# Transposes, ada outputs and row scales at new places in a two-block transformer kernel

## The reference

```
mod = silu(c) @ ada_w + ada_b                 # six rows: shift, scale, gate, twice
h = rmsnorm(x, g1) * (1 + scale_m) + shift_m
x = x + gate_m * token_mix(h)                 # gated linear attention, latent attention (16 heads), a gated sum, @ w_out
h = rmsnorm(x, g2) * (1 + scale_f) + shift_f
x = x + gate_f * ((silu(h @ Wg) * (h @ Wu)) @ w_down)
x = rmsnorm(x, final_norm_g)
```

```
proj = rms_norm(x, pre_g[l]) @ w_in[l]        # retention, differential attention, gated linear recurrence
mixed = [retention * silu, diff_attention * silu, lru * silu]
x = x + rms_norm(mixed @ w_out[l], post_g[l])
```

## Time and profile before

| | us |
|---|---|
| median of 3 runs | 2756.21 (2754.75 to 2757.06) |
| profiled execution | 2750.28 |
| its span | 2748.5 |
| mean granted TensorE clock | 0.989 of full |
| PE busy | 2605.1 |
| DVE, ACT busy | 1757.0, 1295.9 |

### The profile page before, as it was taken

One profiled execution on the slowest core, in us unless ns is written; L12 is line 12 of the kernel. 1 busy time (PEld: TensorE's weight loads), 2 busy tenths in 40 slices (PEclk: granted clock), 3 DMA queues, 4 the chain that ended last, 5 costly groups with the idle time before them and its releaser, 6 DMA issues.

```text
span 2748.5 us, 36054 instructions
## 1 busy us (share of the span) xinstructions
PE 2605.1 (95%) x13167; PEld 2202.0 (80%) x13167; DVE 1757.0 (64%) x2417; ACT 1295.9 (47%) x1885; POOL 69.8 (3%) x110
## 2 busy tenths in 40 slices
PE   2898999899999999899999999999999999999998
PEld 2787887788878778788888888888887887878886
DVE  5887776776666665677765555565666555566654
ACT  2334344534555444544443444445645544565553
POOL 0000000000000000000000000002000000200000
PEclk9999999999999999999999999999999999999999
DMA  9875666788656567577776666656565465656464
GB/s 338 281 258 175 192 192 189 222 280 282 210 179 191 181 223 224 183 256 248 246 230 194 190 188 186 189 179 174 158 185 167 124 220 142 182 161 181 134 198 140
DMA packets 341690, 554.82 MB, mean 202 GB/s; under 512 B 24590, under 2 KB 135932, under 8 KB 340876
## 3 DMA queue, kind: packets, MB, share of 16 engines
q1 hardware_dynamic: 335616, 541.79, 62.6%
q0 software_dynamic: 3280, 7.64, 0.9%
q10 hardware_dynamic: 2620, 3.09, 0.3%
HBM read 550.35 MB, written 2.10 MB: 201 GB/s over the span
## 4 chain that ended last, share of the span: by engine, by line
PE 81%; issue 6%; DVE 5%; ACT 4%; POOL 1%; DVEq 0%; POOLq 0%; ACTq 0%
PE gp L786 72%; PE tp L786 6%; PE tp L789 2%; ACT whi L1194 2%; DVE wlo L1771 1%; POOL stat L2429 1%; DVE acc L1777 0%; ACT rv L1194 0%; ACT L1194 0%; DVE xs L1777 0%; DVE xs L1771 0%; DVE m L1771 0%; DVE yd L1771 0%; DVE sgb L1771 0%; ACT stg L1194 0%
## 5 line engine op out<-in xcount | busy, mean ns | idle before, releaser
L1771 DVE TENSOR_TENSOR wlo<-raw,whi 128x1024 fp32r<-128x1024 f32 (+1 forms) x842 | 989.3, 1188 | 626.4 <-ACT whi L1194 624.5
L1194 ACT ACTIVATE whi<-raw 128x1024 fp32r<-128x1024 f32 (+1 forms) x842 | 852.1, 1029 | 571.3 <-PE gp L786 481.4
L786 PE MATMUL gp<-whi,h 128*128 128x512 f32 (+1 forms) x2944 | 929.4, 388 | 6.6 <-DVE wlo L1771 3.1
L786 PEld LDWEIGHTS gp<-whi,h 128*128 128x128 f32 x2944 | 551.8, 189 | 112.3 <-issue 15.8
L786 PE MATMUL gp<-h,whi 128*128 128x512 f32 (+1 forms) x1936 | 601.9, 370 | 23.4 <-DVE wlo L1771 16.6
L786 PE MATMUL gp<-wlo,h 128*128 128x512 f32 (+1 forms) x1472 | 561.2, 381 | 0.0
L786 PE MATMUL gp<-h,wlo 128*128 128x256 f32 x1680 | 473.6, 282 | 0.0
L786 PEld LDWEIGHTS gp<-h,whi 128*128 128x128 f32 x1936 | 352.8, 192 | 92.4 <-issue 25.7
L786 PEld LDWEIGHTS gp<-h,wlo 128*128 128x128 f32 x1680 | 320.6, 191 | 0.8 <-issue 0.7
L786 PEld LDWEIGHTS gp<-wlo,h 128*128 128x128 f32 x1472 | 278.0, 189 | 45.3 <-issue 1.4
L1777 DVE SCALAR_TENSOR_TENSOR acc<-raw,cact,acc 128x512 f32<-128x512 f32 x298 | 223.3, 749 | 11.4 <-DMA raw<-in_ada_w_dram 4.5
(11 more groups left out here) (318 smaller groups left out, 2704.3 us busy)
## 6 DMA issues: line engine op xcount, KB each, us to landing
raw<-in_w_in_dram SPq DMA_DIRECT2D x314, 512.0 KB, 4.4
raw<-in_ffn_w_in_dram SPq DMA_DIRECT2D x176, 512.0 KB, 4.7
raw<-in_ada_w_dram SPq DMA_DIRECT2D x158, 512.0 KB, 4.6
raw<-in_w_out_dram SPq DMA_DIRECT2D x96, 512.0 KB, 4.4
raw<-in_ffn_w_down_dram SPq DMA_DIRECT2D x88, 512.0 KB, 4.2
raw<-in_w_in_dram SPq DMA_DIRECT2D x64, 384.0 KB, 3.5
raw_first<-in_ada_w_dram SPq DMA_DIRECT2D x34, 512.0 KB, 5.7
raw<-in_gla_wo_dram SPq DMA_DIRECT2D x32, 512.0 KB, 5.4
```

Of the source, the lines that this page charges most:

```text
L786: return e.matmul(o, l, r, start=start, stop=stop)
L1194: return e.activation(o, i, f, **kw)
L1771: return e.tensor_tensor(o, a, b, op)
```

## The change

ada_out, lat_T, mt_T and rp_T get idle steps ahead of them. The last unit of ymla 0 is laid behind the fifth unit of ymla 1. The ada units of `gate_f` stand behind units with n % 7 in (0, 2, 4), and none beside fg 0 and fu 0. f_sc works on 256 columns, two of them ahead of the first transposes. X is multiplied by the final gain alone (`lf_g`, VectorE) a few steps after each hx_T, squared (`lf_sq`, ScalarE), and scaled by the row scale much later on ScalarE (`lf_x` in the chain `lres`); `ls_rn` works the scale in by hand. In retention, the gate products rt_M go one step ahead of the transposes and share steps with them. The squares le_sq move between the transposes. At the end, one half of the tokens is added on PE (X by the identity, y by a diagonal matrix of row scales), and ScalarE copies it out.

```diff
-    for job in [j for j in jobs if not j["chunks"][0]["first"]]:
+    rest = [(job, ci) for job in jobs if not job["chunks"][0]["first"] for ci in range(len(job["chunks"]))]
+
+    late = [u for u in rest if u[0]["name"] == ("ymla", 0) and u[1] == 7]
+    rest.remove(late[0])
+    i = [n for n, u in enumerate(rest) if u[0]["name"] == ("ymla", 1) and u[1] == 4][0]
+    rest[i + 1:i + 1] = late
+    for job, ci in rest:
         kind = job["kind"]
-        for ci in range(len(job["chunks"])):
-            units.append((job, ci))
-            if kind in ("q", "k", "v", "g", "cq", "ckv", "ga", "ygla") and more and n % 2:
-                units.append(more.pop(0))
-            if kind in ("uq", "ukv", "gb", "ymla") and gate_m and n % 3 == 0:
-                units.append(gate_m.pop(0))
-            if kind in ("fg", "fu") and gate_f and n % 3 == 0 and not (job["name"] in (("fg", 0), ("fg", 12)) and ci == 0):
-                units.append(gate_f.pop(0))
-            n += 1
+        units.append((job, ci))
+        if kind in ("q", "k", "v", "g", "cq", "ckv", "ga", "ygla") and more and n % 2:
+            units.append(more.pop(0))
+        if kind in ("uq", "ukv", "gb", "ymla") and gate_m and n % 3 == 0:
+            units.append(gate_m.pop(0))
+        if kind in ("fg", "fu") and gate_f and n % 7 in (0, 2, 4) and job["args"] != (0,):
+            units.append(gate_f.pop(0))
+        n += 1
...
-        return [idle, step(("ada_add", (seq,), 0)), step(("ada_out", (seq, b), 1))]
+        return [idle, step(("ada_add", (seq,), 0)), idle, idle, step(("ada_out", (seq, b), 1))]
...
-        return [idle, step(("lat_T", (name, 0), 1), need=[("gla",)]), step(("lat_T", (name, 2), 1))]
+        return [idle, idle, idle, step(("lat_T", (name, 0), 1), need=[("gla",)]), step(("lat_T", (name, 2), 1))]
...
-        return [idle, step(("mt_T", (j, 0), 1)), step(("mt_T", (j, 1), 1))]
+        return [idle, idle, idle, step(("mt_T", (j, 0), 1)), step(("mt_T", (j, 1), 1))]
...
-        for j in range(4):
-            a = [("f_rn", (), 0), ("f_sc", (0,), 0)] if j == 0 else []
-            b = [("f_sc", (j + 1,), 0)] if j < 3 else []
-            steps += [step(*a, ("f_T", (2 * j,), 1)), step(*b, ("f_hi", (2 * j,), 0)), step(("f_T", (2 * j + 1,), 1)),
-                      step(("f_hi", (2 * j + 1,), 0), *([("f_gfb", (), 0)] if j == 3 else []))]
+        for pair in range(8):
+            first = [("f_rn", (), 0), ("f_sc", (0,), 0), ("f_sc", (1,), 0)] if pair == 0 else []
+            ahead = [("f_sc", (n,), 0) for n in (pair + 2, pair + 3) if pair % 2 == 0 and n < 8] + ([("f_gfb", (), 0)] if pair == 7 else [])
+            steps += [step(*first, ("f_T", (pair,), 1)), step(*ahead, ("f_hi", (pair,), 0))]
...
-        return [idle, step(("hx_T", (2 * j,), 1)), step(("hx_T", (2 * j + 1,), 1))]
+        return [idle, step(("hx_T", (2 * j,), 1)), step(("hx_T", (2 * j + 1,), 1)), idle, step(("lf_g", (j,), 0)), step(("lf_sq", (j,), 0))]
     if kind == "lfirst":
-        return [step(("lf_rn", (), 0), ("lf_x", (0,), 0), need=[("hx", j) for j in range(4)])] + [step(("lf_x", (j,), 0)) for j in range(1, 4)] + \
-            [step(("ls_rn", (0,), 0))]
+        return [step(("lf_rn", (), 0)), step(("ls_rn", (0,), 0), need=[("hx", j) for j in range(4)]), step(("ls_rs", (), 0))]
+    if kind == "lres":
+        return [idle] * 12 + [step(("lf_x", (j,), 0)) for j in range(4)]
...
-        return [step(("rp_r", (kind, l, j, 0), 0), need=[("lru", l)]), step(("rp_r", (kind, l, j, 1), 0)), idle] + \
+        return [step(("rp_r", (kind, l, j, 0), 0), need=[("lru", l)]), step(("rp_r", (kind, l, j, 1), 0)), idle, idle] + \
...
+        steps += [step(("rt_M", (l, which), 0), need=[("evac", "rvg", l, 2)])]
         for h in range(which, 6, 2):
-            steps += [step(("rt_M", (l, h), 0), need=[("evac", "rvg", l, 2)]), step(("rt_T", (l, h), 1))]
+            steps += [step(*[("rt_M", (l, n), 0) for n in range(h + 2, 6, 2)[:1]], ("rt_T", (l, h), 1))]
...
-            return [step(("le_rn", (l,), 0), *[("le_add", (l, j), 0) for j in range(4)])]
+            return [step(("le_rn", (l,), 0), ("le_y", (), 4), *[("le_add", (l, j), 0) for j in range(4)])]
...
-            steps += [step(*a, ("le_T", (2 * j,), 1)), step(*b, ("le_T", (2 * j + 1,), 1))]
-        return steps + [step(("le_sq", (j,), 0)) for j in range(4)] + [step(("ls_rn", (1,), 0))]
+            steps += [step(*a, ("le_T", (2 * j,), 1)), step(*b, ("le_T", (2 * j + 1,), 1), ("le_sq", (j,), 0))]
+        return steps + [step(("ls_rn", (1,), 0))]
...
-                if job["name"] in (("ga", 0), ("uq", 0)):
+                if job["name"] == ("uq", 0):
...
-            for k in job["order"][ci:ci + 2]:
+            for k in job["order"][ci:ci + (1 if (job["name"], ci) == (("ymla", 0), 6) else 2)]:
...
+                if job["name"] == ("ga", 0):
+                    until(("lat", "q"), ("lat", "k"))
...
-            for n in range(2):
-                e.dma_start(o_rows[:, n, cj], X[:, n, cj]).then_inc(d_out, 16)
+            e.dma_start(o_rows[:, 0, cj], X[:, 0, cj]).then_inc(d_out, 16)
+            u = uses["le_y",][j]
+            w.wait_ge(tp_act[u.b], at("tpa", *u))
+            e.dma_start(o_rows[:, 1, cj], X[:, 1, cj]).then_inc(d_out, 16)
...
+        def le_y(us):
+
+            for j, u in enumerate(us):
+                w.wait_ge(x_add, at("x_add", 0, j))
+                mm(empty(u)[:, :], ident, X[:, 1, j * 512:(j + 1) * 512], True, False)
+            w.wait_ge(diag_done, 1)
+            for j, u in enumerate(us):
+                result_dve("w2", 1, j)
+                mm(TP[u.b][:, :], DIAG[:, :], Y[:, 1, j * 512:(j + 1) * 512], False, True).then_inc(tp_full[u.b], 1)
...
+        def lf_sq(us, j):
+
             ss = scol(8, "lf_ss")
             for t in range(2):
-                w.wait_ge(x_done, at("x_done", j, t))
+                w.wait_ge(x3g_done, at("x3g", j) - 1 + t)
                 if j:
-                    w.wait_ge(ss_done, at("ss", "lf_x", j - 1, t))
+                    w.wait_ge(ss_done, at("ss", "lf_sq", j - 1, t))
                 fn(XQ[:, t, :], X[:, t, j * 512:(j + 1) * 512], ACT.Square, accum=ss[:, 4 * t + j:4 * t + j + 1]).then_inc(ss_done, 1)
-                note(ss_done, "ss", "lf_x", j, t)
+                note(ss_done, "ss", "lf_sq", j, t)
+
+        def lf_x(us, j):
+            w.wait_ge(pow_out, at("pow", "lf"))
+            w.wait_ge(ss_done, at("ss", "lf_sq", j, 1))
+            for t in range(2):
+                x = X[:, t, j * 512:(j + 1) * 512]
+                copy(x, x, scale=scol(2, "lf_rs")[:, t:t + 1]).then_inc(x_done, 1)
+            note(x_done, "x_done", j)
...
-        def f_sc(us, j):
+        def f_sc(us, pair):
             w.wait_ge(pow_out, at("pow", "f"))
-            cj = slice(j * 512, (j + 1) * 512)
+            cp = slice(pair * S, (pair + 1) * S)
             for t in range(2):
-                ts(XN[:, t, cj], X[:, t, cj], scol(2, "f_rs")[:, t:t + 1], None, ALU.mult).then_inc(xnf_done, 1)
+                ts(XN[:, t, cp], X[:, t, cp], scol(2, "f_rs")[:, t:t + 1], None, ALU.mult).then_inc(xnf_done, 1)
...
+        def lf_g(us, j):
+
             w.wait_ge(d_gfb, 16)
-            read(first_use("hx_T", 7))
             cj = slice(j * 512, (j + 1) * 512)
+            read(first_use("hx_T", 2 * j + 1))
             for t in range(2):
-                stt(X[:, t, cj], X[:, t, cj], scol(2, "lf_rs")[:, t:t + 1], GFB[:, cj], ALU.mult, ALU.mult).then_inc(x_done, 1)
-                note(x_done, "x_done", j, t)
+                w.wait_ge(ss_done, at("ss", "dn", j, t))
+                tt(X[:, t, cj], X[:, t, cj], GFB[:, cj], ALU.mult).then_inc(x3g_done, 1)
+            note(x3g_done, "x3g", j)
...
+            tt(sq, r, r, ALU.mult).then_inc(dve_self, 1)
+            own()
+            w.wait_ge(ss_done, at("ss", "lf_sq", 3, 1))
+            for n in range(2):
+                e.reduce_sum(ss[:, n:n + 1], scol(8, "lf_ss")[:, 4 * n:4 * n + 4], AX_X).then_inc(dve_self, 1)
+                v = own()
+            w.wait_ge(dve_self, v)
+            tt(ss, ss, sq, ALU.mult).then_inc(dve_self, 1)
+            w.wait_ge(dve_self, own())
+            rms(ss, D, ("rs", 0), ("ls", 0))
...
 
+        def le_y(us):
+            ts(DIAG[:, :], ident, scol(2, "le_rs", 1)[:, 1:2], None, ALU.mult).then_inc(diag_done, 1)
...
-            for n in range(2):
+            for n in range(2 if l == 0 else 1):
                 stt(X[:, n, cj], Y[:, n, cj], scol(2, "le_rs", l)[:, n:n + 1], X[:, n, cj], ALU.mult, ALU.add).then_inc(x_add, 1)
```

More of the change, by code:

```diff
@@ L448, in step @@
                     done.add(("layer", 0))
+                    launch("lres")
                 if sid[0] == "lend" and sid[1] == 0:
@@ L463, in stat_need @@
         if s == "hf":
-            return [("ffn", 4 * (k // 4) + (1 if k % 4 < 2 else 3))]
+            return [("ffn", k // 2 * 2 + 1)]
         if s in ("lq", "lk"):
-            return [("lat", s[1], 1 + k // 2)]
+            return [("lat", s[1], 3 + k // 2)]
```

(22 more changed lines are left out.)

22 lines of the change are left out of this document (10 added, 12 removed).

## The result

Six runs of the changed kernel have a median of 2747.4 us, six of the kernel before 2755.2: a ratio of 0.9972 (0.9960 to 0.9983), 7.7 us or 0.28% faster. Forecast were 22 us and a time of 2734; the range began at 2725 and ended at 2745. The sign was right, the size wrong by two thirds. The profiled executions differ by even less, 2745.7 against 2748.5 of span.

The account below looks back on a forecast made before the run. PE, busy 95% of the span, was taken as the bound, so only its idle and slow-clock time could be won. Terms summed to 22 us, taken from the median 2756.2: 2734 us, range 2725 to 2745.

Parts of the forecast that it names:

- ymla: Last chunk of ymla 0 moved behind the fifth of ymla 1: saves idle time and slow clock, gain 4.9 us.
- mt: mt transposes two steps later: all four waits on m and slow clock behind one go, gain 6.3 us.
- layer border: Residual scaling at the layer border moved to ScalarE, squares spread apart: PE's idle there shrinks, gain 3.3 us.
- lat: Latent transposes later: wait on stg and its slow clock go, 0.5 us stays for a late wlo; gain 4.4 us.
- ada_out two steps later: Adaptive-norm sums: waits of PE on them shrink, 2.0 us gained at 492 and 1.5 elsewhere; gain 3.5 us.
- The FFN's start: First FFN transposes: a weight split makes VectorE wait on whi and PE idle 3 us; loss 3.2 us.
- rival 2: Low clock holds longer at the FFN's start, 3 us more than in the sum: 2737 us, chance 0.17.
- gate_f denser: Three ada chunks per seven product chunks in the FFN: extra load hidden under PE, gain or loss nothing.
- rival 4: Raw-buffer ring limits fg and fu transfers to 241 GB/s or less: 2759 us, 2770 at 230; chance 0.03.
- Rope and retention: Idle step before rp_T gains 0.5 us; retention's reordered gate products gain 0, the 5.8 on rg stays.
- The end: Final additions split between VectorE and PE, ScalarE copying out: finishes earlier, gain 1.2 us, bounds 0 and 2.
- Rival 1: Half of the first four parts' 19.1 us comes back as waits on wlo: 2744 us, chance 0.15.

Follow-up runs that it names:

- best_v2: Changed kernel with the old gate_f rule, old rp_T idle count and early ada_out, plus two idle steps ahead of retention's first rt_M: median 2729.8 us, ratio 0.9911.
- u_ffn: Changed kernel with the old steps at the FFN's first transposes (512-wide scalings), new gate_f rule kept: span 2741.8 us, ratio 0.9971.
- u_gate: Changed kernel with the old gate_f rule back (ada chunks behind every third product chunk, beside fg 0 too): median 2737.4 us, ratio 0.9944.

## Why the prediction was wrong, step by step

Three terms had the mechanism wrong: the later ada_out (3.5 forecast as gained, 3.0 lost), the denser gate_f (nothing forecast, 3.4 lost and more with PE's pace) and the end (1.2 forecast, nothing gained). The idle step ahead of rp_T cost 1.0 a layer instead of gaining 0.25.

- **ymla, mt, layer border:** right in mechanism and size: 4.0 for 4.9, 6.0 for 6.3, 4.2 for 3.3. Behind ymla a wait of 1.8 on sx stays in which the forecast saw nothing; with the early ada_out it is 0.45 and the gain 5.4. At the border the waits of rows 10 are gone to the last.
- **lat:** right in mechanism. The stg wait of rows 4 and its low clock go whole: from 514 to 530 the changed kernel gains 5.3 us, best_v2 5.2, against 4.4 and a bound of 4.9. The 0.5 that I left for a late wlo did not come.
- **ada_out two steps later:** wrong in sign, 3.5 forecast, -3.0 measured. The step that failed: I priced the waits on the sums alone, as if two idle steps put ada_out two chunks later and left all other chains where they were, at no cost. But the next sum needs this one gone, and `until` forces it out by sweeps without a product, as I had described it for pair 7 under ymla. At 13 of 16 sums ada_out comes behind the same chunk as without the idle steps, and what moves is the other chains, forward. The 2.4 on kf with 1.5 of low clock behind it, the 2.0 at the pairs and 1.4 of the sx wait are that. The sum at 492 does go later, by one chunk: 1.1 gained of 2.93, not 2.0.
- **The FFN's start:** right in mechanism, to the instruction: wlo behind the first transposes, VectorE waiting on whi, scalings 2 and 3 behind it, PE idle 3.14 between the second and the third pair. 4.5 instead of 3.2: the low clock held through all of the first chunk (0.53, in the row below). That is rival 2 in kind, with 1.3 us of its 3. The narrower scalings gave the first transposes their 0.27 (5.50 for the 5.77 of rows 8), and by u_ffn nothing else.

```profile
1120.20:1124.70 4.50, 4.50 (x17) 3.88 (x16) 2.52 (x7) 2.80 (x6) 0.00 (x0) 0.53 0.18 65
```

  The Trainium skill, TensorE: Matmul & The Clock Gate, Part 1, has the throttled clock as the default and activity as its release; the row agrees, PE having been idle for 5.50 and 3.14 us with 2 us of transposes between.
- **gate_f denser, "nothing; hidden under PE":** the other step that failed, at 3.4 us of its own in a stretch that lost 3.4 to 5.5. I compared means over a turn, 2.3 us of VectorE in 2.77. A fu evacuation is a burst: four operations of it, then two additions to the sum, and three splits are late in a row, in the changed kernel:

```profile
1242.49 0.69 DVE L1808 TENSOR_TENSOR sl<-sl,ul 128x512 f32<-128x512 f32 x1
1243.88 0.69 DVE L1808 TENSOR_TENSOR al<-sl,ah 128x512 fp32r<-128x512 f32 x1 [0.70 <-ACT ah L1217]
1244.49 1.53 DVE L1814 SCALAR_TENSOR_TENSOR acc<-raw,cact,acc 128x512 f32<-128x512 f32 x2
1245.94 3.49 DVE L1808 TENSOR_TENSOR wlo<-raw,whi 128x1024 fp32r<-128x1024 f32 x3
...
1247.30 0.47 PE L799 MATMUL gp<-h,whi 128*128 128x512 f32 x1 [0.65 <-DVE wlo L1808]
```

  Transfers were not it: rival 4 is out, with 245, 269 and 238 GB/s in the changed kernel from 1150 to 1400 where the kernel before moved 247, 250 and 255:

```profile
1150.00:1230.00 80.00, 78.86 (x447) 68.06 (x446) 59.99 (x75) 36.46 (x48) 0.76 (x1) 1.00 0.76 245
1230.00:1310.00 80.00, 79.35 (x452) 68.37 (x451) 59.84 (x75) 38.03 (x51) 0.97 (x2) 1.00 0.82 269
```

  The three waits make 3 to 3.4 us by their matmuls' delay; the rest is PE's pace (last section). u_ffn, which has the same three waits and never runs at the slow pace there, lost 3.40; the changed kernel's two profiles, with about 100 and 40 us at the slow pace, 5.47 and 4.25. The pace isn't the rule's doing: u_gate, without the rule, has it too, from 1136 to 1186.
- **Rope and retention:** the 5.8 on rg stayed, as forecast. The idle ahead of rp_T was to gain 0.25 a layer and cost 1.0. Nothing is forced here; what I left out is the chain behind it: the retention's scores come a chunk later, where rvg's evacuation is in their way (the 1.14 on rat). The clock put 1.5 on top of it where the first profile of the kernel before had none.
- **le_sq:** the wait of rows 11 went, 1.25 us by the delay of its matmuls, for 1.2; what is more in the table is clock behind the 4.8 us wait on xs, as the kernel before's own second profile shows (-1.49).
- **The end:** right in the compute (0.7 shorter), wrong in what ends last: the transfers, which I priced at nothing. Gained were 0.0 of 1.2.
- **Rivals:** none as written. Rival 1 said that 9.5 of the 19.1 of the first four parts comes back as waits on wlo. 12.2 came (3.65 + 0.47 - 1.98 + 4.02 + 6.00), so 6.9 did come back, but on kf, pt and sx, by the forced sweeps, and 1.5 of it as clock behind kf.
- **The profiled time against the median:** I took 5.9 us between them as an offset that carries over. It was the luck of one execution; the changed kernel's profile has none of it (2747.5 against 2747.4).

Open: why PE's pace in the ffn product locks at one value or the other, whether the order of the work shifts the odds of the low clock behind rg, and whether ada_out can be moved at 492 alone without the others; none was tried.

## What to carry to other kernels

In a hand-made plan an idle step ahead of something that a later unit needs may leave its own step where it was and move all the others: the planner forces that chain to its end, and the other chains come forward with it. Print the order before and after and look at each pair of steps that came closer, before pricing the one that was meant to move. Price an added load at the worst burst of the engine that takes it, not at its mean over a turn, and look at what will stand in an engine's queue between two of its urgent instructions: one that waits for nobody is harmless there, one that waits for another engine is not. For a gain of a few us take two profiles of the kernel before, since the clock behind a wait comes and goes by itself.
